# Stick-breaking attention: VectorE caps the scores two units ahead of its softplus, TensorE issues the scores three units ahead

## What is computed

```python
z = jnp.einsum('bhqd,bhkd->bhqk', q_blk, kt).astype(jnp.float32) * scale
mask = key_pos[None, :] < q_pos[:, None]
log_not = jnp.where(mask, jax.nn.log_sigmoid(-z), 0.0)
between = lax.cumsum(log_not, axis=3, reverse=True) - log_not
a = jnp.where(mask, jnp.exp(jax.nn.log_sigmoid(z) + between), 0.0)
return jnp.einsum('bhqk,bhkd->bhqd', a.astype(vt.dtype), vt)
```

## Time and profile before

| what | value |
|---|---|
| time, median of 3 runs | 2257.37 us (2255.98 to 2260.44) |
| profiled execution, its own time | 2260.76 us |
| its span | 2259.0 us |
| TensorE busy, of the span | 2069.8 us (92%) |
| mean granted TensorE clock of the span | 0.968 of 2.4 GHz |
| the stage, from 950.0 to 1089.5 us of the span | 139.5 us, TensorE busy 112.55, ScalarE 70.00, VectorE 55.60, GpSimd 50.26 |

### The profile page before, as it was taken

How to read it: one execution, slowest core, us unless ns; L and a number is a source line. 1 busy time by engine, 2 the same in 40 slices (tenths; PEclk the granted TensorE clock), 3 DMA queues, 4 the chain that set the end, 5 groups by cost and what they waited for, 6 DMA issues and landing times. The chain is left out here.

```text
span 2259.0 us, 28394 instructions
## 1 busy us (share of the span) xinstructions
PE 2069.8 (92%) x11594; PEld 1633.6 (72%) x11594; DVE 1161.6 (51%) x1426; ACT 863.7 (38%) x1243; POOL 331.2 (15%) x310
## 2 busy tenths in 40 slices
PE   8999888799988879988889999999998889999996
PEld 4777876477787658733668888877888776888884
DVE  3545645454654553243468547636333748845753
ACT  4236432523643251255344324423122625423431
POOL 0200723020071320033220000021000011000002
PEclk9999899899989989999999999999999989999998
DMA  5211011221201113210212222223221012223221
GB/s 214 75 72 60 3 62 51 94 76 56 75 2 39 75 58 111 81 41 1 75 67 87 93 100 100 83 91 125 96 97 53 1 38 79 102 90 110 96 78 62
DMA packets 30406, 167.51 MB, mean 74 GB/s; under 512 B 2795, under 2 KB 9379, under 8 KB 14660
## 3 DMA queue, kind: packets, MB, share of 16 engines
q1 hardware_dynamic: 30276, 165.68, 20.4%
HBM read 159.34 MB, written 10.00 MB: 75 GB/s over the span
## 5 line engine op out<-in xcount | busy, mean ns | idle before, releaser
L258 PE MATMUL psum<-inputs_high,weights_high 128*128 128x512 f32 x928 | 377.6, 407 | 16.6 <-DVE inputs_low L239 9.7
L260 PE MATMUL psum<-inputs_high,weights_low 128*128 128x512 f32 x928 | 362.6, 391 | 0.0
L259 PE MATMUL psum<-inputs_low,weights_high 128*128 128x512 f32 x928 | 362.4, 391 | 0.0
L1857 PE MATMUL psum<-inputs_high,weights_high 128*128 128x512 f32 x704 | 275.9, 392 | 9.2 <-DVE inputs_low L1995 9.2
L244 DVE TENSOR_TENSOR weights_low<-weights_raw,weights_high 128x2048 fp32r<-128x2048 f32 x72 | 169.1, 2350 | 208.3 <-ACT weights_high L233 208.3
L1858 PE MATMUL psum<-inputs_low,weights_high 128*128 128x512 f32 x704 | 274.0, 389 | 0.0
L1859 PE MATMUL psum<-inputs_high,weights_low 128*128 128x512 f32 x704 | 274.0, 389 | 0.0
L258 PEld LDWEIGHTS psum<-inputs_high,weights_high 128*128 128x128 f32 x928 | 174.4, 188 | 70.9 <-DVE inputs_low L239 14.2
L233 ACT CAST weights_high<-weights_raw 128x2048 fp32r<-128x2048 f32 x72 | 136.7, 1898 | 207.2 <-PE psum L260 193.1
L259 PEld LDWEIGHTS psum<-inputs_low,weights_high 128*128 128x128 f32 x928 | 174.8, 188 | 38.0 <-issue 4.3
L260 PEld LDWEIGHTS psum<-inputs_high,weights_low 128*128 128x128 f32 x928 | 174.6, 188 | 37.4
(11 more groups left out here) (334 smaller groups left out, 3302.5 us busy)
## 6 DMA issues: line engine op xcount, KB each, us to landing
weights_raw<-w_stream SPq DMA_DIRECT2D x116, 1024.0 KB, 4.8
weights_raw<-w_down SPq DMA_DIRECT2D x32, 704.0 KB, 4.0
residual_parked<-residual SPq DMA_DIRECT2D x2, 2048.0 KB, 9.7
residual_back<-residual_parked SPq DMA_DIRECT2D x2, 2048.0 KB, 7.8
residual<-x_t SPq DMA_DIRECT2D x1, 2048.0 KB, 7.7
bias_by_row<-bias_rows SPq DMA_DIRECT2D x2, 1024.0 KB
out_t<-residual SPq DMA_DIRECT2D x8, 256.0 KB, 2.0
bias_by_row<-bias_rows SPq DMA_DIRECT2D x1, 1536.0 KB
```

The lines of the kernel that those rows point to most:

```text
L258: pe.matmul(out, hi, self.ahi[:, k], start=start and b == 0, stop=False)
L259: pe.matmul(out, hi, self.alo[:, k], start=False, stop=False)
L260: mm = pe.matmul(out, lo, self.ahi[:, k], start=False, stop=stop and b == blocks - 1)
L1857: pe.matmul(out, wh, hi, start=start, stop=False)
```

## The change

VectorE caps units 0 and 1 first, and then does `softplus(u)`, `cap(u + 2)`; for this `z_capped` gets a third buffer. TensorE issues the scores of units 0, 1 and 2 first, and then `sums(u)`, `values(u - 1)`, `scores(u + 3)`. Since the PSUM slots are still three, `scores(u + 3)` goes into the slot that `sums(u)` has just completed, and waits for `weights(u)`. The orders of ScalarE and GpSimd, and all shapes, stay as they are.

```diff
@@ stick_attention
-        zc = stack.enter_context(sbuf(nc, "z_capped", [P, 2, 2, T], F32))
+        zc = stack.enter_context(sbuf(nc, "z_capped", [P, 3, 2, T], F32))
@@ block.tensor
-                for u in range(n_units + 2):
+                for u in range(3):
+                    scores(u)
+                for u in range(n_units + 1):
                     if u < n_units:
-                        scores(u)
-                    if 1 <= u <= n_units:
-                        sums(u - 1)
-                    if u >= 2:
-                        values(u - 2)
+                        sums(u)
+                    if u >= 1:
+                        values(u - 1)
+                    if u + 3 < n_units:
+                        scores(u + 3)
@@ block.vector, cap(u)
-                    if u >= 2:
-                        dve.wait_ge(s.log, u - 1)
-                        dve.wait_ge(s.softplus, u - 1)
-                    dve.tensor_scalar(zc[:, u % 2, :, jt * P:], zbank(u)[:, :, jt * P:], 40.0, None, ALU.min) \
+                    if u >= 3:
+                        dve.wait_ge(s.log, u - 2)
+                        dve.wait_ge(s.softplus, u - 2)
+                    dve.tensor_scalar(zc[:, u % 3, :, jt * P:], zbank(u)[:, :, jt * P:], 40.0, None, ALU.min) \
                         .then_inc(s.capped, 1)
@@ block.vector
-                for u in range(n_units + 1):
-                    if u >= 1:
-                        softplus(u - 1)
-                    if u < n_units:
-                        cap(u)
-                    if u >= 6 and (u - 6) % TT == 0:
-                        copy_out((u - 6) // TT)
+                cap(0)
+                cap(1)
+                for u in range(n_units):
+                    softplus(u)
+                    if u + 2 < n_units:
+                        cap(u + 2)
+                    if u >= 5 and (u - 5) % TT == 0:
+                        copy_out((u - 5) // TT)
                 copy_out(pairs - 1)
```

More of the change, by code:

```diff
@@ L1716, in softplus @@
                         dve.wait_ge(s.later, 2 * made_later(u - 1))
-                    dve.tensor_tensor(softp[:, u % 2, :, jt * P:], zbank(u)[:, :, jt * P:], zc[:, u % 2, :, jt * P:],
+                    dve.tensor_tensor(softp[:, u % 2, :, jt * P:], zbank(u)[:, :, jt * P:], zc[:, u % 3, :, jt * P:],
                                       ALU.max).then_inc(s.softplus, 1)
@@ L1735, in logs @@
                     jt = units[u][1]
-                    z = zc[:, u % 2, :, jt * P:]
+                    z = zc[:, u % 3, :, jt * P:]
                     act.wait_ge(s.capped, u + 1)
```

## The result

| | before | after |
|---|---|---|
| time, median | 2258.9 us (4 runs) | 2245.68 us (4 runs, 2245.44 to 2248.95) |
| ratio | | 0.9944, 95% interval 0.9927 to 0.9962 |
| profiled execution, span | 2259.0 us | 2247.2 us |
| the stage, first scores to the next stage's first matmul | 139.5 us | 126.1 us |
| a steady pair of heads | 16.49 us | 15.25 us |

The change makes the kernel 0.56% faster; 2245.2 us were forecast. The kernel before now has a fourth run, which lifts its median from 2257.4, from which the forecast was counted, to 2258.9. The profiled execution after is the slowest of its four runs. Against the profile before, its stage is 13.5 us shorter and starts 1.6 us earlier, while everything behind the stage, which the change does not touch, takes 3.3 us more (1172.7 against 1169.4).

The account below looks back on a forecast made before the run. The bound was taken as the line cap, Exp, Ln, softplus plus the 256 cap's wait for scores. Savings of 11.2 and 1.0, together 12.2 us, off the 2257.4 median gave 2245.2 us, range 2240 to 2251.

Parts of the forecast that it names:

- What bounds before: VectorE always works or waits in a steady pair: 6.91 busy, 5.9 for Ln, 3.4 for scores, 16.2 of 16.49 us.
- The new ring: Sums(u), weights(u), scores(u + 3), sums(u + 1) through TensorE and ScalarE: 14.60 us a pair, 15.27 with one stall.
- The stall of the 384 sums: TensorE waits there for the mask, as the 384 softplus stands behind the 512 cap and bank copy: 0.67 us a pair.
- Units 3 to 31: Stretch from unit 3's sums to unit 31's: from 117.10 to 105.9 us, a saving of 11.2.
- Units 0 to 3: Stage start, first sums to unit 3's: from 12.44 to 11.45 us (8.95 plus 2.5 for low clock), saving 1.0.
- The second low-clock stretch: TensorE at 1.2 GHz from 965.7 to 968.9 us, costing about 1.6 us; expected gone after the change.
- Rival 4, the clock: TensorE's halts for ScalarE and the mask drop its clock: 2258 us at once a pair, 2271 at twice; chance 0.03.

Follow-up runs that it names:

- The dose on the weights: One extra ScalarE copy out of PSUM ahead of each weights instruction: on the changed kernel 2250.25 us, on the kernel before 2260.67 us.
- the last experiment: Kernel before with TensorE's scores three ahead and weights done head by head, VectorE in its order of before: 2244.17 us, ratio 0.9934.
- The first experiment: Changed kernel with TensorE's loop of before, so only VectorE's cap order and third z_capped buffer are new: 2334.4 us, ratio 1.033.

## Why the prediction was right, and where it was off

- **What bounds before** (cap, Exp, Ln, softplus in a line, and once a pair the scores behind the 512 sums): the chain is shown as a whole, but not that both parts had to go. That Ln's wait fell from 47.2 to 9.9 us is no proof of it: with TensorE's half alone that wait was 66.6 us, and the steady pair was 15.23 all the same. The place of the scores by itself is enough to take the pair from 16.49 to there. The forecast let both parts go together and gave neither a price. Its time does not hang on this, since the ring and one stall are the bound either way. The dose on the weights, which cost the kernel before nothing, shows that the ring was not yet the bound there.
- **The new ring**, 5.25, 2.71, 3.36 and 3.95, 15.27 us: measured 5.23, 2.71, 3.38 and 3.93, 15.25. The dose shows that it is a ring through ScalarE's weights, in the two places where neither the values nor the stall cover it, behind the 512 and the 384 sums. The unseen release from ScalarE to TensorE, taken as 0.07, is 0.05 to 0.06.
- **The stall of the 384 sums** behind 512 cap and copy, 0.67: measured as 0.62 of idle time, and removed by moving the copy.
- **Units 3 to 31**, 105.9: 105.72.
- **Units 0 to 3**, the mis-sized term: 1.0 us was to be saved and 2.1 were. The step was "I expect that again", of a low-clock stretch as long as before, 6.9 us, which would add 2.5 to 8.95. It was 3.4 us long (953.55 to 956.95) and cost 10.31 - 8.95 = 1.4, nearly all of it between the sums of units 1 and 2 (4.04 for the 2.76 of the forecast). Why it was shorter was not tested; what the trace shows is that the new order gives TensorE its third block of scores before the first sums, and that it stood idle for 1.46 us there instead of 2.10. In the profile of TensorE's half alone, with the same early scores, the low stretch was again some 6.8 us long, so the early scores alone do not explain it. Over the other kernels, one profile each, the stretch is 6.8 to 6.9 us long in the kernel before, in the kernel before with the dose and in TensorE's half alone, 3.3 to 3.4 in the changed kernel, with the copy moved, with the dose, with the scores ahead of the values and in the last experiment, some 10 in VectorE's half alone, and it is absent in the other two kernels with weights by head. The cause stays open.
- **The second low-clock stretch** was expected to go, and went: the clock is 1.00 from 965 us to the end of the stage.
- **Rival 4, the clock**: not in this kernel, where TensorE idles 0.6 us at most in steady pairs. The first experiment shows the clock falling in another order of the same work, with idle stretches of up to 3.3 us. The Trainium skill, "TensorE: Matmul & The Clock Gate", section "A second HAM failure mode: psum-queue depth-cycling", warned of short idles between groups of matmuls; here idles of 0.3 to 0.6 us left the clock at 1.00, and the rule did not come to bear. The same page of the Trainium skill, section "HAM oscillation — how this bites in real kernels", tells of a matmul loop that falls back to the low clock at each long wait for a DMA. The first experiment fits it in kind, with waits for VectorE's softplus and its mask in place of the DMA: the longest was 3.31 us, and the clock fell in every pair.

In total 12.2 us were forecast and 13.2 measured between the medians, 13.5 in the profiled stage. The time itself came out only 0.5 us over the forecast by luck: the saving was 1.0 us larger than forecast, and the median that it is taken from rose by 1.5 with its fourth run.

## What to carry to other kernels

When a pipeline over several engines is deepened, its next bound is a ring through the buffers that were not multiplied: here the three PSUM slots, freed by ScalarE. Its length can be worked out from the old trace block by block, with the handovers, and each other engine's line is then held against it; that found both the gain and the one stall, and the stall's cause was the next improvement. A lead on one engine is of no use, and can cost much, if what it runs ahead on is issued late by another: the same cap order cost 76 us without the scores ahead. And work that is put into a wait must stand ahead of the waiting instruction: the values behind the scores cost nearly the whole gain.

## What the runs showed that was not expected

- With idle stretches of up to 3.3 us between TensorE's blocks the clock fell to 1.2 GHz in every pair, and an expected loss of 48 us became 76. Idles up to 1.3 us in the steady pairs of the kernel before, and 1.11 in the order with scores ahead of values, left it at 2.4.
- A ScalarE copy of 128x256 elements out of PSUM lasts 0.38 us in the trace, but costs 0.28 in a row of instructions without waits between them.
